# Two layer norms and a router: statistics taken beside the mixer's output products, rows of routed tokens made token-wise

## The reference

```python
    mix = hybrid_mixer(h, ...)
    x = layer_norm(DEEPNORM_ALPHA * x + g_m * mix, ln_mix_g, ln_mix_b)
    h = layer_norm(x) * (1.0 + sc_f) + sh_f
    ffn = grouped_moe(h, w_router, b_router, w1, w3, w2)
```

```python
    probs = softmax(h @ w_router)            # 16 experts in 4 groups
    sel = probs + b_router
    # best group by the sum of its two largest sel, then its two largest experts
    # each token's row of h is placed in the block of each of its two experts
```

## Time and profile before

| | us |
|---|---|
| median of 3 runs (2815.69 to 2827.67) | 2826.22 |
| the profiled execution's own time | 2821.1 |
| its span in the trace | 2819.3 |
| TensorE busy in the span | 2566.3 |

### The profile page before, as it was taken

How to read it: one execution, slowest core, us unless ns; L and a number is a source line. 1 busy time by engine, 2 the same in 40 slices (tenths; PEclk the granted TensorE clock), 3 DMA queues, 4 the chain that set the end, 5 groups by cost and what they waited for, 6 DMA issues and landing times. The chain is left out here.

```text
span 2819.3 us, 32901 instructions
## 1 busy us (share of the span) xinstructions
PE 2566.3 (91%) x12907; PEld 2007.5 (71%) x12907; DVE 1756.1 (62%) x2552; ACT 1124.6 (40%) x1599; POOL 46.7 (2%) x148
## 2 busy tenths in 40 slices
PE   7999899999999989499996798899997988899998
PEld 6677677677777776278884255688886986688886
DVE  6878734486776664489994465667767473643334
ACT  4433232235455322478882234441324244351323
POOL 0000000000000000100001000000000000000000
PEclk8999799999999999799998899999998898999998
DMA  7666636222221842299993112234332224223221
GB/s 253 215 224 203 222 121 258 69 75 68 60 60 60 293 155 90 120 343 416 415 399 112 51 54 62 70 105 139 122 106 86 99 45 164 75 90 101 94 90 30
DMA packets 289718, 409.90 MB, mean 145 GB/s; under 512 B 21704, under 2 KB 209595, under 8 KB 279964
## 3 DMA queue, kind: packets, MB, share of 16 engines
q1 hardware_dynamic: 281724, 377.91, 39.1%
q0 software_dynamic: 5392, 20.97, 1.9%
q10 hardware_dynamic: 2448, 8.91, 0.8%
HBM read 368.96 MB, written 38.80 MB: 145 GB/s over the span
## 5 line engine op out<-in xcount | busy, mean ns | idle before, releaser
L3366 PE MATMUL banks<-big,late_parts 128*128 128x512 f32 x1920 | 442.8, 392 | 11.1 <-DVE late_parts L3539 7.3
L3366 PEld LDWEIGHTS banks<-big,late_parts 128*128 128x128 f32 x1920 | 363.2, 189 | 89.1 <-DVE late_parts L3539 7.5
L3366 PE MATMUL banks<-h_parts_second,late_parts 128*128 128x512 f32 x1440 | 332.5, 391 | 12.8 <-DVE h_parts_second L3563 12.8
L3366 PEld LDWEIGHTS banks<-h_parts_second,late_parts 128*128 128x128 f32 x1440 | 271.9, 189 | 70.9 <-issue 14.4
L3539 DVE TENSOR_TENSOR late_parts<-w_second,late_parts 128x2048 fp32r<-128x2048 f32 x69 | 158.0, 2292 | 218.5 <-ACT late_parts L3428 218.3
L2270 DVE TENSOR_TENSOR expert_parts<-w,expert_parts 128x2048 fp32r<-128x2048 f32 x102 | 233.1, 2289 | 34.4 <-ACT expert_parts L2266 33.3
L1317 PE MATMUL banks<-h_parts,ssm_parts 128*128 128x512 f32 x984 | 243.0, 405 | 6.6 <-DVE ssm_parts L1613 6.1
L3428 ACT ACTIVATE late_parts<-w_second 128x2048 fp32r<-128x2048 f32 x69 | 132.0, 1914 | 255.4 <-PE banks L3366 255.4
L1317 PEld LDWEIGHTS banks<-h_parts,ssm_parts 128*128 128x128 f32 x984 | 188.8, 195 | 54.8 <-DVE ssm_parts L1613 7.9
L2266 ACT ACTIVATE expert_parts<-w 128x2048 fp32r<-128x2048 f32 x102 | 195.0, 1916 | 65.5 <-PE banks L2277 65.4
L2277 PE MATMUL banks<-expert_parts,expert_xt 128*128 128x512 f32 x816 | 195.4, 399 | 5.0 <-DVE expert_xt L2640 5.0
(11 more groups left out here) (649 smaller groups left out, 3835.5 us busy)
## 6 DMA issues: line engine op xcount, KB each, us to landing
w_second<-in_mlp_w_dram SPq DMA_DIRECT2D x64, 1024.0 KB, 5.1
w<-in_w_exp_gate_dram SPq DMA_DIRECT2D x34, 1024.0 KB, 7.7
w<-in_w_exp_up_dram SPq DMA_DIRECT2D x34, 1024.0 KB, 7.4
w<-in_w_exp_down_dram SPq DMA_DIRECT2D x34, 1024.0 KB, 8.7
w<-in_w_in_dram SPq DMA_DIRECT2D x65, 512.0 KB, 3.8
w<-in_mod_mix_w_dram SPq DMA_DIRECT2D x24, 1024.0 KB, 4.9
w<-in_mod_ffn_w_dram SPq DMA_DIRECT2D x24, 1024.0 KB, 4.9
w<-in_w_in_dram SPq DMA_DIRECT2D x16, 1024.0 KB, 6.4
```

What stands on the lines that cost most here:

```text
L3366: mm = pe.matmul(ps[:, bank(n, f), :], w_part(n, w)[:, kk, f * P:(f + 1) * P], x[:, v, kk, :], start=(first_chunk(n) and kk == 0 and j == ...
```

## The change

The two `norm_stage` calls of the first block are gone, and with them `k.h`. Their work is spread over the stages before and behind.

In `residual_stage` the factor alpha is applied by ScalarE ahead (8 instructions), so that one VectorE instruction takes a tile out of its bank. A `TokenNorm` gathers the first norm's statistics beside the products: a first sum and a product for a shift after the second half row, shifted tiles, running sums of tiles and of squares. The last half row gives its two tiles one after the other. Six products by ones follow the last half row, then mean, variance and inverse root; the inverse root is written into bank 3. SP stores two rows of the modulation (shift and scale of the second norm) to DRAM, element by element, and loads the router's weights, which GpSimd multiplies by the scale.

In `routing_stage` the first norm is finished tile by tile (`scaled`, `affine`). As tiles come, TensorE transposes them token-major and multiplies them, as stationary operand, with a matrix of 17 columns (the weighted router and a column of ones), so that logits and sums are born token-major. ScalarE squares the transposed tiles with an accumulator for the second variance. Mean and inverse root of the second norm are then `[128, 4]` and enter the logits afterwards. The rows of token block 0 are made by TensorE (`rows_of`: a diagonal product and a two-row product), those of blocks 1 to 3 by VectorE with two instructions each, behind the slots. The first expert's weights are now loaded at the start of this stage, behind two broadcasts of the stored rows.

```diff
-def norm_stage(k, name, dst, scale, shift, sum_next=False, also=None, room=None, experts=None, logits=False, ahead=None):
+def norm_stage(k, name, dst, scale, shift, also, ahead):
...
 def residual_stage(...)
+            for j in range(2):
+                sp.dma_start(mod_rows[j:j + 1, :].rearrange("o (c p) -> p (o c)", p=P), k.mod[:, first + j * KD:first + (j + 1) * KD],
+                             allow_slow_non_contiguous=True).then_inc(s["rows_stored"], 16)
+            router.load(sp, s["router_loaded"])
+            sp.wait_ge(s["rows_stored"], 32)
...
             for n in range(N):
-                halves.products(pe, base + n, x_parts, [ps[:, n * HT + f, :] for f in range(HT)], arriving=(s["x_low"], 0) if n == 0 else None)
-            sum_channels(k, pe, lambda c: pe.wait_ge(s["vec_step"], 2 * (c + 1)))
+                outs = [ps[:, n * HT + f, :] for f in range(HT)]
+                if n < N - 1:
+                    halves.products(pe, base + n, x_parts, outs, arriving=(s["x_low"], 0) if n == 0 else None)
+                else:
+                    halves.product(pe, base + n, 0, x_parts, outs[0], final=False).then_inc(s["seventh_done"], 1)
+                    halves.product(pe, base + n, 1, x_parts, outs[1], final=True)
+                if n == 1:
+                    norm.pe_shift(pe)
+            norm.pe_sums(pe)
...
 def routing_stage(...): SP
+            for j in (1, 0):
+                sp.dma_start(both_b[:, j, :], mod_rows[j:j + 1, :].to_broadcast([P, D])).then_inc(s["wide_loaded"], 16)
+            sp.dma_start(row_pair[:], mod_rows).then_inc(s["rows_loaded"], 16)
+            for h in range(EH):
+                m.load(sp, 0, h)
...
 TensorE
+            for kk in range(KD):
+                pe.matmul(ps[:, 2, P:P + WIDE], k.ones[:], wide[:, kk, :], start=(kk == 0), stop=(kk == KD - 1))
+            for c in range(KD):
+                pe.wait_ge(s["x_ready"], c + 1)
+                for b in range(TB):
...
+                    mm = pe.transpose(ps[:, y_bank(n), c % 4 * P:(c % 4 + 1) * P], k.x[:, c, b * P:(b + 1) * P], k.ident[:])
...
+                if c >= 2:
+                    logits_of(c - 2)
...
 VectorE
             dve.tensor_scalar(m.slots[1][:], g[1][:], -1.0, None, ALU.add).then_inc(s["slots_ready"], 1)
+            for b in range(ON_PE, TB):
+                u, row = room[:, b % 2, :], ht[:, b, :].rearrange("p (k c q) -> p c q k", k=KD, c=KD)
+                step(dve.scalar_tensor_tensor(out=u, in0=scale_b, scalar=pair[:, b, 1:2], in1=shift_b, op0=ALU.mult, op1=ALU.add))
+                natural = lambda v: v.rearrange("p (c q k) -> p c q k", c=KD, k=KD)
+                dve.scalar_tensor_tensor(out=row, in0=natural(ys[:, b, :]), scalar=root[:, b:b + 1], in1=natural(u), op0=ALU.mult,
+                                         op1=ALU.add).then_inc(s["rows_ready"], 1)
...
-                    norm_stage(k, "norm_mix", k.x, lambda c: k.col("ln_mix_g", c), lambda c: k.col("ln_mix_b", c), sum_next=True, room=room,
-                               experts=experts)
-                    norm_stage(k, "norm_ffn_in", k.h, mod(32), mod(24), room=room, experts=experts, logits=True)
-                    routing_stage(k, experts)
+                routing_stage(k, experts, mod_rows, router)
```

More of the change, by code:

```diff
@@ L497, in _ @@
             k.clear(sp)
-            if experts and not logits:
-                experts.load_router(sp)
-                for h in range(EH):
-                    experts.load(sp, 0, h)
-            if ahead:
-                ahead(sp)
+            ahead(sp)
         @block.tensor
@@ new lines, in affine @@
+            def affine(c):
+                act.wait_ge(s["scaled"], c + 1)
+                act.activation(k.x[:, c, :], k.x[:, c, :], ACT.Identity, scale=k.col("ln_mix_g", c), bias=k.col("ln_mix_b", c)).then_inc(s["x_ready"], 1)
+            for c in range(5):
+                affine(c)
+            act.wait_ge(s["bias_ready"], 1)
+            for c in range(5, KD):
+                squares(c - 5)
+                affine(c)
+            for n in range(3, 2 * TB):
+                squares(n)
+            act.wait_ge(s["var_ready"], 1)
@@ L2385, in _ @@
+            dve.scalar_tensor_tensor(out=pair[:, :, 1], in0=mean[:], scalar=-1.0, in1=root[:], op0=ALU.mult, op1=ALU.mult).then_inc(s["pair_ready"], 1)
             dve.wait_ge(s["exp_done"], 1)
```

265 lines of the change are left out of this document (199 added, 66 removed).

## The result

The changed kernel takes 2804.27 us (median of 4 runs, 2797.22 to 2806.09), the kernel before 2825.95 us beside it. The ratio is 0.9932, 95% interval 0.9911 to 0.9953. The forecast was 2807 us with a range from 2797 to 2817.

What follows compares the result with a forecast made beforehand. It took a single chain of waits, 88.85 us from the mixer's last product to the experts' first transpose, as the bound. New terms start the experts at 1173.6 instead of 1190.5, 16.9 us gained: 2807 us, range 2797 to 2817.

Steps and rivals of the forecast that it cites:

- The residual stage: Mixer's end: shift product adds 0.9 us, closing sums to exponential 8.64 us, alpha and running sums hidden; routing starts at 1111.5.
- TensorE in the routing stage: Routing up to logits: 80 passes at 0.205 and 32 transposes at 0.246, 24.3 us at the lower clock; logits at 1136.0.
- The reason that it gave for the clock: Routing stage: TensorE idles some 3 us across the barrier, then finds only narrow work; hence passes of 0.205 us.
- From `sel` to the slots: Routing, selection to slots: old chain of 13.06 us stays, plus 0.3 charged for new TensorE row work; slots at 1152.2.
- VectorE behind the slots: Routing's end: three row blocks 8.8 us (strided write 1.6 each), small instructions 2.7, four subtractions 8.9; ends at 1172.6.
- one of its signs of being wrong: VectorE's row work in the routing stage: strided instructions taking over 2 us would show the prediction wrong.
- The scatters: GpSimd at the routing stage's end: last scatter 1163.7, rows landed 1170.1, ahead of VectorE, so no term but a rival.
- A: Rival, routing stage: clock granted fully, TensorE needs 13.1 us, ScalarE is last; 6 us more gain, 2801; chance 0.14.
- B: Rival, routing's end: slow scatters, strided write 2.56 us or narrow passes 0.24, 3 us each; 2811 to 2815; chance 0.32.
- C: Rival, experts' start: something taken as hidden, such as broadcasts then weights, holds the stage; gain below 5 us, 2818; chance 0.04.
- D: Rival, residual stage: element-wise store outlasts its stage, landing some 72 us after issue or later; 2825 to 2835; chance 0.03.
- The base: Whole kernel: gain taken from profiled 2821.1 gives 2804.2, from median 2826.2 gives 2809.3; forecast 2807 between them.

Runs made afterwards that it cites:

- residual_only: Kernel before plus only the new residual stage, first norm finished in a short stage of its own; 2809.12 us against 2821.74 before, ratio 0.996.
- fill_the_barrier: Changed kernel plus eight unused 512-column products by ones behind the residual stage's closing sums; experts' first transpose at 74.51 us against 70.72 in the changed kernel.
- wide_logits: Changed kernel with the router's products 512 columns wide (16 passes instead of 64), then turned; logits at 31.06 us against 32.64, first transpose 69.14 against 70.72.
- wide_early: Changed kernel with 512-column router products from the first tile on, constant products at the end; logits at 29.07 us against 32.64, first transpose 67.15 against 70.72.
- no_rows_on_pe: Changed kernel with all four token blocks' rows on VectorE, none on TensorE and ScalarE; slots at 48.47 us against 49.00, first transpose 73.19 against 70.72.
- no_vector_rows: Changed kernel without the six VectorE instructions that make the rows of blocks 1 to 3; experts' first transpose at 69.22 us against 70.72.

## Why the prediction was right

Point by point, by its own steps:

- **The residual stage.** The closing sums to the exponential took 8.39 us where the last stage's norm had promised 8.4, and the shift product 0.86. Alpha's instructions and the running sums were indeed hidden: from the first mixer product to the first closing one it was 46.89 us against 45.67, of which 0.86 is the shift product. The 0.4 us left over are hardly a term: in the other runs with this stage the same piece took 46.5 to 46.9. residual_only shows this half to be worth 9.6 us.
- **TensorE in the routing stage.** The clock was 0.50, as forecast, and TensorE was busy for 23.4 of the 24.0 us to the logits, where the forecast had 24.3 without a wait. A tile of four transposes and eight narrow passes took 2.45 us (1121.78 to 1124.23), where the forecast's prices give 4 x 0.246 + 8 x 0.205 = 2.62. The logits were ready 0.6 us before the forecast. The reason that it gave for the clock had two parts, idle time at the barrier and narrow work behind it; fill_the_barrier shows that the first isn't needed, and wide_logits and wide_early that the second keeps the clock from coming back. VectorE had 20 wide instructions beside it, not the 12 that the forecast counted (it left out the eight that scale the transposed tiles); it had room all the same.
- **From `sel` to the slots.** 13.70 us against 13.06 + 0.3. The ranks' products did wait behind the half row, 0.5 us (no_rows_on_pe).
- **VectorE behind the slots.** The strided instruction took 2.00 us on average (2.02, 2.01 and 1.97), at the bound of 2.0 that the forecast named, not the 1.6 that it took. Over 2 us was one of its signs of being wrong, and this stands on the line: the term was taken too small, and cost 0.6 us, three blocks in 9.4 us and not 8.8. Logits and `sel` had come 0.7 us early, which made up for it; that the sum fits to 0.1 us is luck.
- **The scatters.** I called GpSimd no term, and it wasn't one. The forecast had both chains: by the landing alone the experts could start at 1170.1, by VectorE at 1173.6, 3.5 us apart. Measured it is 68.1 and 70.72 on the scale of the table, 2.6 us apart. What the forecast didn't say is how little of VectorE's row work this leaves to be gained: without all 9.4 us of it the stage ends 1.5 us earlier (no_vector_rows), and GpSimd with the landing is what ends it then.
- **The rivals.** A did not occur (clock 0.50 from 0.6 us into the stage). Of B the strided write was dearer by 0.4 us a piece, not by 0.96, and the eight scatters took 12.4 us, not 8 x 2.2 = 17.6. Beside VectorE's row instructions they were slow only in part: of the six, four took 1.49 to 1.88 us and two 0.95. Three of the slow ones started in the midst of a strided instruction and ended 0.70 to 0.73 us behind its end (1150.71 + 1.49 against 1149.45 + 2.02), the two fast ones started about 0.1 us ahead of one. C and D did not occur: the broadcasts landed 4.8 us after their issue, and the store 10.3 us after its own.
- **The base.** I placed the forecast between profiled execution and median. The stretch gave 17.0 us, the medians differ by 21.7, the interval reaches from 13 to 25; the 4.7 us between are not explained by any step (so that 2804.27 lies so near to 2807 is in part luck), and the positions of the first closing product show that a single execution moves by more.

## What to carry to other kernels

Read the end of a stage as two or three chains of known length, not as one: an edit on the longest gains only down to the next, and the releaser in the bracket of the first instruction behind (barrier or landing) tells which it was. Work that waits at a stage's end is better put into idle time of the same engines earlier in the stage (2.5 us gained) than on GpSimd beside VectorE (1.5 us lost). And where many narrow products replace few wide ones, price them at TensorE's lower clock, and try the wide form in more than one order: to the logits it gained 1.6 us in the first order and 3.6 in the second.

## What the runs showed of the hardware

- A VectorE instruction of 0.22 us took 4.53 us beside a GpSimd subtraction of 4.50 us on other data. The Trainium skill, "GPSIMD Engine Reference", Key points, names SBUF interfaces that the two engines share, and contention when VectorE has two SBUF inputs; the trace agrees, and here the wait was as long as GpSimd's whole instruction (one run, one instruction).
- TensorE's clock stood at 0.50 for 23 us in which it was busy almost without a gap with products of 17 columns and transposes of 128. In the same stage it came back to 1.00 when products of 512 columns took turns with the transposes (wide_early), and when the transposes followed one another with no 17-column passes between them (wide_logits).
- A store of two rows in pieces of one value landed 10.3 us after its issue and held the load behind it as long; in pieces of eight values 1.7 us.
- A write with a stride of 128 values cost VectorE 1.55 times a plain one (1997 against 1285 ns).
- An indirect scatter took GpSimd 0.95 us by itself and mostly 1.9 beside VectorE's long subtractions, which have two SBUF inputs.
